# Convolution history behind the masked probabilities, tails stored one group sooner, two groups of the last down projection interleaved, in a one-core decoder step

## The reference, cut to what matters

```python
def _causal_dwconv(x, buf, w):               # buf: the history, width-1 rows
    xx = jnp.concatenate([buf.astype(x.dtype), x], axis=1)
    y = xx[:, 0:t] * w[0]
    for i in range(1, width):
        y = y + xx[:, i:i + t] * w[i]
    return y, xx[:, -(width - 1):]           # the last rows are an output: the tail

# token mixing, one projection h @ w_in feeds both branches
qkv, gdn_buf_new = _causal_dwconv(qkv_raw, gdn_buf, p["w_gdn_conv"])
o_gdn, s_new = _gated_delta_chunked(gq, gk, gv, log_alpha, beta, gdn_s0)
p = jax.nn.softmax(s, axis=-1)               # sparse attention, branch B
o = jnp.einsum('bqkgj,bqjkd->bqkgd', p.astype(v_sel.dtype), v_sel)

# channel mixing
u, ffn_buf_new = _causal_dwconv(jnp.dot(h2, p["w_up"]), ffn_buf, p["w_ffn_conv"])
x = x + gt2 * jnp.dot(jax.nn.silu(u_gate) * u_val, p["w_down"])   # w_down: 5632 x 2048
```

## Time and profile before

| what | value |
|---|---|
| three runs | 1954.58, 1957.79 and 1961.79 us; median 1957.79 us |
| the profiled execution | span 1957.9 us |
| PE | 1888.0 us busy, 96% of the span, 16742 matmuls |
| POOL | 1186.2 us, 61% |
| ACT | 801.3 us, 41% |
| DVE | 638.5 us, 33% |
| loaded and stored | 390.69 MB, mean 200 GB/s |
| mean granted TensorE clock | 0.977 of full speed |

### The profile page before, as it was taken

How to read it: one execution, slowest core, us unless ns; L and a number is a source line. 1 busy time by engine, 2 the same in 40 slices (tenths; PEclk the granted TensorE clock), 3 DMA queues, 4 the chain that set the end, 5 groups by cost and what they waited for, 6 DMA issues and landing times.

```text
span 1957.9 us, 41659 instructions
## 1 busy us (share of the span) xinstructions
PE 1888.0 (96%) x16742; PEld 1763.5 (90%) x16742; DVE 638.5 (33%) x1782; ACT 801.3 (41%) x1345; POOL 1186.2 (61%) x508
## 2 busy tenths in 40 slices
PE   6799999998999999999999899999999999999997
PEld 1299989998888878888999899999999999999996
DVE  1355634542223331423352433321033321123333
ACT  1444346644223232322433655543344443344432
POOL 0075646663444434434877577777777777777773
PEclk8699999999999999999999999999999999999999
DMA  9966434444787878787855345454454444445452
GB/s 392 409 230 208 151 114 146 146 167 142 236 303 248 283 250 281 253 290 260 244 189 169 129 163 170 162 168 165 164 169 162 169 163 167 166 164 169 161 172 87
DMA packets 145102, 390.69 MB, mean 200 GB/s; under 512 B 27522, under 2 KB 36162, under 8 KB 144322
## 3 DMA queue, kind: packets, MB, share of 16 engines
q1 hardware_dynamic: 124976, 374.01, 56.1%
q10 hardware_dynamic: 19986, 14.70, 2.4%
HBM read 379.70 MB, written 8.88 MB: 198 GB/s over the span
## 4 chain that ended last, share of the span: by engine, by line
PE 89%; DMA 5%; DVE 2%; issue 1%; ACT 1%; POOL 1%; DVEq 0%; ACTq 0%; SPq 0%; POOLq 0%; PEldq 0%
PE bank L2243 27%; PE bank L2244 26%; PE bank L2248 25%; PE bank L2218 3%; DMA raw_a<-in_stream 3%; DMA raw_c<-in_stream 1%; PE bank L2727 1%; PE bank L2194 1%; PE bank L2207 0%; DMA out_gdn_tail_p<-cpt 0%; DMA raw_b<-in_stream 0%; DMA raw_m<-in_stream 0%; PE bank L2596 0%; PE bank L2612 0%; PE bank L2311 0%
## 5 line engine op out<-in xcount | busy, mean ns | idle before, releaser
L737 POOL TENSOR_TENSOR rest_a<-raw_a,hi_a 128x1024 fp32r<-128x1024 f32 x174 | 417.6, 2403 | 349.7 <-ACT hi_a L795 349.7
L2243 PE MATMUL bank<-h_hi,hi_a 128*128 128x288 f32 x1752 | 485.5, 303 | 1.9 <-ACT hi_a L795 1.8
L2244 PE MATMUL bank<-h_lo,hi_a 128*128 128x288 f32 x1752 | 474.5, 296 | 0.0
L2243 PEld LDWEIGHTS bank<-h_hi,hi_a 128*128 128x128 f32 x1752 | 331.8, 189 | 20.2 <-issue 16.7
L2244 PEld LDWEIGHTS bank<-h_lo,hi_a 128*128 128x128 f32 x1752 | 332.7, 190 | 0.4
L795 ACT ACTIVATE hi_a<-raw_a 128x1024 fp32r<-128x1024 f32 x174 | 184.2, 1059 | 299.9 <-PE bank L2248 221.9
L737 POOL TENSOR_TENSOR rest_b<-raw_b,hi_a 128x1024 fp32r<-128x1024 f32 x78 | 187.5, 2403 | 121.5 <-ACT hi_a L795 121.5
L2248 PE MATMUL bank<-h_hi,rest_a 128*128 128x288 f32 x1544 | 236.2, 295 | 2.8 <-POOL rest_a L737 2.8
L2248 PEld LDWEIGHTS bank<-h_hi,rest_a 128*128 128x128 f32 x1544 | 216.1, 189 | 3.0 <-POOL rest_a L737 3.0
L737 POOL TENSOR_TENSOR rest_a<-raw_a,hi_b 128x1024 fp32r<-128x1024 f32 x56 | 134.1, 2394 | 61.3 <-ACT hi_b L795 61.3
L2243 PE MATMUL bank<-h_hi,hi_b 128*128 128x288 f32 x616 | 169.2, 301 | 0.0
(11 more groups left out here) (511 smaller groups left out, 3742.8 us busy)
## 6 DMA issues: line engine op xcount, KB each, us to landing
raw_a<-in_stream SPq DMA_DIRECT2D x376, 512.0 KB, 3.5
raw_b<-in_stream SPq DMA_DIRECT2D x185, 512.0 KB, 3.8
raw_c<-in_stream SPq DMA_DIRECT2D x94, 512.0 KB, 3.3
raw_m<-in_stream SPq DMA_DIRECT2D x29, 512.0 KB, 6.2
st<-in_state ACTq DMA_DIRECT2D x8, 512.0 KB, 5.7
st<-in_state SPq DMA_DIRECT2D x8, 512.0 KB, 5.8
out_state_s<-st ACTq DMA_DIRECT2D x8, 512.0 KB, 6.8
x<-in_x SPq DMA_DIRECT2D x2, 1152.0 KB, 13.6
```

What stands on the lines that cost most here:

```text
L737: nc.gpsimd.tensor_tensor(rest_in(name, r), raw_of(name, r), w_hi[q].bitcast(f32), ALU.subtract).then_inc(lo_ready, 1)
L2243: MM(banks[c][:, 0:N], w_, hi_of(k), start=(first and k == 0), stop=False)
L2244: ins = MM(banks[c][:, 0:N], w_, lo_of(k), start=False, stop=False)
```

## The change

Three edits. In DVE's loop over n, `history()` stands behind `mask_p(u)` instead of ahead of it. The two stores of the convolution's tails are issued in the iteration n = 24, behind the first `hi_in` of it, instead of behind the loop. And in `dn2` the six slots of groups 0 and 1 run in the order (0,0) (0,1) (1,0) (1,1) (0,2) (1,2), written (group, slot), instead of (0,0) (0,1) (0,2) (1,0) (1,1) (1,2); `last_down` gives the position of each, the loads are issued in that order, and who waits for a group waits for its new last slot.

```diff
--- before.py
+++ after.py
@@ -170,6 +170,14 @@
 assert _b == NSLOTS
 
 
+def last_down(m, s_):
+
+    k = SUPERS[-1][1]
+    if m >= 2:
+        return k * m + s_
+    return (k - 1) * m + s_ if s_ < k - 1 else 2 * (k - 1) + m
+
+
 def ffn_slots():
 
     per, up_of = 4 * (KT // KS) + KT // CT, (0, KT // KS, 2 * (KT // KS) + KT // CT, 3 * (KT // KS) + KT // CT)
@@ -179,9 +187,11 @@
             for q in range(4):
                 at = BASE["ffn"] + (q * (KT // KS) if c == 0 else per * c - KT // CT + up_of[q])
                 out += [at + k for k in range(KT // KS)]
-        for m in range(KT // CT):
-            for c in range(first, first + count):
-                out.append(BASE["last"] + m if c == NCH - 1 else BASE["ffn"] + per * c + 3 * KT // CT + m)
+        order = [(m, c) for m in range(KT // CT) for c in range(first, first + count)]
+        if first + count == NCH:
+            order.sort(key=lambda mc: last_down(mc[0], mc[1] - first))
+        for m, c in order:
+            out.append(BASE["last"] + m if c == NCH - 1 else BASE["ffn"] + per * c + 3 * KT // CT + m)
     return out
 
 
@@ -564,6 +574,8 @@
 
             if name == "go":
                 j, per_j = 2 * g + 1, 2 * per
+            elif name == f"dn{len(SUPERS) - 1}":
+                j, per_j = last_down(g, SUPERS[-1][1] - 1), 0
             elif name[:2] == "dn":
                 k = SUPERS[int(name[2])][1]
                 j, per_j = k * g + k - 1, k * per
@@ -1013,6 +1025,10 @@
                 else:
                     conv_w3(n - 1)
                 hi_in(j)
+                if n == N_IN - 1:
+                    act.wait_ge(conv_w, QKV_T // CT)
+                    act.dma_start(O["gdn_tail_s"], ctl[:, :, :].rearrange("p t n -> p (t n)")).then_inc(out_done, 16)
+                    act.dma_start(O["gdn_tail_p"], cpt[:, :, :].rearrange("p t n -> p (t n)")).then_inc(out_done, 16)
                 if n == 1:
                     rows_a()
                 if n == 2:
@@ -1069,11 +1085,6 @@
                     first_norms()
 
 
-            act.wait_ge(conv_w, QKV_T // CT)
-            act.dma_start(O["gdn_tail_s"], ctl[:, :, :].rearrange("p t n -> p (t n)")).then_inc(out_done, 16)
-            act.dma_start(O["gdn_tail_p"], cpt[:, :, :].rearrange("p t n -> p (t n)")).then_inc(out_done, 16)
-
-
             def pair_norm(u):
 
                 act.wait_ge(G["o"], u + 1)
@@ -1808,14 +1819,14 @@
                     scores_part(u)
                 if u == 0:
                     mask_q(1)
-                if n == N_QKV - 1:
-                    history()
                 if N_QKV <= n - 1 < N_IN - 1:
                     conv_taps(n - 1)
                 if n - 1 == N_IN - 2:
                     mix_clear()
                 if 0 <= u < KV:
                     mask_p(u)
+                if n == N_QKV - 1:
+                    history()
                 if 0 <= u < UNITS:
                     out_part(u)
                 if n == N_IN - 4:
@@ -2763,6 +2774,14 @@
             norm_end(1)
 
             ah, al = (lambda k: act_hi[:, k, :]), (lambda k: act_lo[:, k, :])
+
+            def down_slot(dn, m, s_, first, count):
+
+                bs, _ = grp(dn, 2, m)
+                pe.wait_ge(act_ready, 2 * (first + s_) + 2)
+                slot(dn, last_down(m, s_), lambda k: ah(s_ * KS + k), lambda k: al(s_ * KS + k), (bank[2 * bs], bank[2 * bs + 1]),
+                     s_ == 0, s_ == count - 1)
+
             for n, (first, count) in enumerate(SUPERS):
                 up, dn = f"up{n}", f"dn{n}"
                 if n == 0:
@@ -2777,7 +2796,14 @@
                         for m in range(2):
                             group(dn, 2, m, count * m, count, ah, al, i, 2, 2 * count, chunk=first)
                 else:
-                    for m in range(KT // CT):
+                    for m in range(2):
+                        bs, cnt = grp(dn, 2, m)
+                        pe.wait_ge(grp_free[bs], cnt + 1)
+                        for s_ in range(count - 1):
+                            down_slot(dn, m, s_, first, count)
+                    for m in range(2):
+                        down_slot(dn, m, count - 1, first, count)
+                    for m in range(2, KT // CT):
                         group(dn, 2, m, count * m, count, ah, al, chunk=first)
             gathered_part(2)
             for s_ in range(KT - CT, KT):
```

## The result

| | kernel before | changed kernel |
|---|---|---|
| median | 1959.79 us (4 runs, 1954.58 to 1962.43) | 1941.57 us (4 runs, 1940.12 to 1946.05) |
| profiled execution's span | 1957.9 us | 1938.3 us |
| its mean granted clock | 0.977 | 0.981 |

The ratio of the times is 0.9917, 95% interval [0.9903, 0.9931]: 0.83% faster, 13.5 to 19.0 us (16.3 us by the ratio, 18.2 by the bare medians of four runs each). Timed again with five more runs in a later session, the changed kernel took 1942.9 us against 1958.78 us, 0.9918 [0.9904, 0.9931]. The forecast was 1939.3 us in a range of 1935 to 1946.

The account below looks back on a forecast made before the run. PE, busy 96% of the span, was the bound; time could come only from its idle 4% and half-clock stretches behind. 6.7 + 8.3 + 3.6 = 18.6 us off 1957.9 gave 1939.3 us, range 1935 to 1946.

Parts of the forecast that it names:

- 0.2 to 0.3 lost: Behind A1: PE at 488.3 needs bt_s, ready at 488.5, so 0.2 to 0.3 us of the tails' gain is lost.
- far behind ACT's 470: Mixing stage's first slot: a load a microsecond late is covered, as PE needs it only after transposes at 478.05 to 478.65.
- lower end of 6.0: Tails: gain only 6.0 us if DVE's chain before bt_s moves 5 us only, by meeting POOL's subtractions.
- ends of 14.0 and 21.0: Whole change: lowest gain 5.0 + 6.0 + 3.0 = 14.0 us (1943.9), highest 7.7 + 9.5 + 3.8 = 21.0 us (1936.9).
- A: Unit 1: one more history instruction meets a POOL subtraction, out_part 2.1 us later, gain 2.6, time 1943.4; chance 0.08.
- B: Mixing stage: DVE's chain or an unlanded slot stops PE 3 us, tails bring some 3 us, time 1944.6; chance 0.08.
- C: Mixing stage: slower, loads run dry without PE's stop; eight waits make 28.8 us, time 1968; chance 0.03.
- D: Later stages: it does nothing, what is gained is waited for at a load later, time 1957; chance 0.03.

Follow-up runs that it names:

- e2: Only the two stores of the tails moved into n = 24, against the kernel before: 1951.58 us (6 runs), ratio 0.9965.
- e3: Only the first six slots of dn2 interleaved, against the kernel before: 1953.58 us (12 runs), ratio 0.9976.
- e1: Only the history moved behind the masked copies, against the kernel before: 1952.55 us (9 runs), ratio 0.9971.
- e5: The changed kernel again, unaltered, on a second chip, against the kernel before: 1942.9 us (5 runs), ratio 0.9918.
- e4: The kernel before with matmuls whose result nobody reads put into the three waits, against the kernel before: 1955.47 us (12 runs), ratio 0.9988.
- e10: Changed kernel with history behind out_part, tail stores ahead of the last group's first hi_in, and token_rows in two pieces, against the kernel before: 1940.99 us, ratio 0.991.

## Why the prediction was right

**Edit 1** was to bring 6.7 us and brought 6.34: PE waits 1.09 us in front of L2437 (1.0 foreseen), and goes on at 274.05. The kernel before runs 0.9 us behind this one at that place, so this is 274.95 by its clock, where 274.7 had been worked out. What had been taken on one row only, that products with two inputs in SBUF stand while POOL subtracts, is now shown on products of 192 columns: 0.34 us alone, 1.76 and 2.55 us beside a subtraction. The section "SBUF: two separate sides" of the Trainium skill's "SBUF — State Buffer" says the same; the trace agrees. One thing was luck within this: the price of the idle time varies. From unit 0's turning back to unit 1's the kernel before took 24.21 us and e2 24.16, but e3, which is the same there, 22.81, as the clock came back sooner. So the edit is worth 4.9 to 6.3 us by the execution it is compared with, and the medians of e1 and of before lie 5.4 us apart.

**Edit 2** was to bring 8.3 us and brought 7.23. The stretch itself came out nearly as worked out, 4.90 us of wait and 9.19 - 5.93 = 3.3 us of clock (3.7 foreseen): 8.2 of the 8.6. The step that was mis-sized is the last: "0.2 to 0.3 lost" at `bt_s` was 0.95. I had moved DVE's chain as a block by 7.4 us. Its head did move by that much, but `bt_s` moved by 6.4 only: L1924 stood for ACT's exponential and began 0.4 us later in the chain than before, and `btc`, which I had left at its old 1.33 us, met POOL's subtraction for longer and took 2.00. (The old 1.33 had some 0.5 us of the same standing in it, which I had not seen.) Both came late because the load beside the stores landed 1.2 us later. The prediction did see that the load could come a microsecond late and priced it only at the slot that it feeds, "far behind ACT's 470": in front of PE it was covered, in front of DVE it was not. The meeting with POOL had been named too, as the reason for the lower end of 6.0; its size fell between. Here as well the kernel before was profiled in a dear execution: from its first transposes (478.05) to those that need `bt_s` (496.87) it took 18.82 us, e1 17.83 and e3 17.65 for the same work, and the changed kernel 11.60. So edit 2 is worth 6.1 to 7.2 us by the execution.

**Edit 3** was to bring 3.6 and brought 3.58, and group 0's and 1's residuals, 3.17 us apart, delayed nothing. Its price did not vary: the three slots behind the second took 13.2 us in the kernel before, in e1 and in e2.

**The sum.** The stages between gave back 0.2 us where I had said none. So 17.0 us are the edits' and the forecast said 18.6; the profiled pair shows 19.6 only with 0.9 us of start and 1.6 us of clock at `token_rows`, which went the changed kernel's way in this pair and cost it 3.4 us in e5. With the cheaper executions of the same stretches the edits come to 14.4 instead of 17.0. The ratios of the times say 16.3 and 16.1 us in the two sessions, which lies between; the forecast's 18.6 lies above both, inside its ends of 14.0 and 21.0.

That the time hit as well as it did has some luck in it. The prediction took the span of 1957.9 us as the same thing as the median time of 1957.79; as a time it is some 1959.7, which is above the medians of 1957.4 to 1958.8 that 9 to 27 runs of the kernel before gave later. A start that was too high and a gain that was too large met at 1941.1, beside the measured 1941.57.

**The rivals.** A did not come true: it needed one more instruction of the history in a subtraction of POOL than the two I had counted, and there were two, ahead of `out_part`. B came in small: DVE's chain did take the place of the wait, with 0.95 us and not 3. C and D are out: the mixing stage gave back 0.2 us, and PE is busy all 40 us between 520 and 560, with the DMA engines at 87%.

## What to carry to other kernels

When a stall goes, price what follows it with the clock that a busy PE has: in the three places 1.5 to 3.3 us of the loss were the matmuls behind the wait, and e4's trace has them back with useless work alone (its time fell by 2.5 us). When a transfer is moved next to a load, follow that load to everything that is behind it on other engines, not only to the matmul that reads it; here it went over ACT's rounding and POOL's subtraction into a VectorE instruction of another chain. And compare two profiles at the same instructions, and more than one profile of the kernel before: 2.5 of the 19.6 us between these two were not made by the change, and up to 2.6 more hang on which execution of the kernel before was profiled.

## What was not expected of the hardware

- The granted clock fell to 0.50 without any idle time of PE, behind 2.8 us of narrow matmuls of 8 rows, in 9 of 12 profiles, and in one (e10) three times behind 2.1 us of matmuls of 128 rows by one column. Behind `token_rows` each time cost 1.7 or 3.4 us, at a place where the waits list shows nothing. In other executions of the same program nothing was lost behind the same pieces.
- The same wait costs a different amount of clock: 24.21 and 22.81 us for the same stretch with a wait of 4.8 us in it. Near 700 us every profile has a wait of 1.9 us for `pd`; behind it the granted clock fell to 0.50 in 9 of the 14 and stayed at 1.00 in 5.
- A load of 512 KB that lands in 3.2 to 3.3 us in six profiles took 4.44 to 4.65 us with stores of 0.32 MB issued in the microsecond before it, and 4.37 once without them.
